# A projection product's bank goes back into the ring of accumulator banks two turns later

## The reference, cut to what matters

```python
proj = h @ w_in[l]                       # h: 512 x 1024
qkv = silu(centred_depthwise_conv(concat([qd, kd, vd]), dn_conv_w[l]))   # 5 taps along the sequence
qd, kd, vd = split(qkv)                  # 512 features each
qd = l2norm(qd per head) * DN_DK**-0.5
kd = l2norm(kd per head)
o  = bidir_gated_deltanet(qd, kd, vd, beta, g)     # 8 heads, chunks of 64
```

## Time and profile before

| | us |
|---|---|
| median of 3 runs | 3446.06 |
| lowest, highest | 3445.08, 3454.87 |
| the profiled execution | 3454.78 |
| its span, first to last instruction | 3453.0 |
| PE busy in it | 3298.4 (96%) |
| DVE busy | 1882.4 (55%) |
| ACT busy | 1437.2 (42%) |

### The profile page before, as it was taken

One profiled execution on the slowest core, in us unless ns is written; L12 is line 12 of the kernel. 1 busy time (PEld: TensorE's weight loads), 2 busy tenths in 40 slices (PEclk: granted clock), 3 DMA queues, 4 the chain that ended last, 5 costly groups with the idle time before them and its releaser, 6 DMA issues.

```text
span 3453.0 us, 61428 instructions
## 1 busy us (share of the span) xinstructions
PE 3298.4 (96%) x26780; PEld 2625.2 (76%) x26780; DVE 1882.4 (55%) x2834; ACT 1437.2 (42%) x2518; POOL 200.7 (6%) x188
## 2 busy tenths in 40 slices
PE   8899999999998999999999998989999999999999
PEld 6587887788875787878788876767788767677787
DVE  6565657756565565557755654453444644434444
ACT  5534224434255443234433454444433445444432
POOL 0041330000000232300000000000000000000000
PEclk9999999999999999999999998999999999999999
DMA  4001103232331011123223231201122312111222
GB/s 153 25 21 45 39 27 123 93 104 92 97 113 49 8 33 50 33 69 117 92 95 101 81 118 47 95 30 63 55 89 78 109 48 89 44 58 59 78 73 95
DMA packets 75212, 249.15 MB, mean 72 GB/s; under 512 B 9280, under 2 KB 10944, under 8 KB 73920
## 3 DMA queue, kind: packets, MB, share of 16 engines
q1 hardware_dynamic: 74944, 245.22, 21.7%
HBM read 237.88 MB, written 6.29 MB: 71 GB/s over the span
## 4 chain that ended last, share of the span: by engine, by line
PE 85%; DVE 7%; ACT 6%; issue 2%; DMA 0%; SPq 0%; ACTq 0%; DVEq 0%
PE psum L518 82%; PE psum L695 2%; ACT s_tmp L1247 1%; ACT s_w L1247 1%; DVE s_nm L2033 1%; DVE s_tmp L1954 1%; DVE s_ffy L1954 1%; DVE s_w L1951 1%; ACT s_E L1247 1%; DVE s_tmp L1951 1%; ACT L1247 0%; DVE s_xb L1951 0%; PE psum L605 0%; ACT L1259 0%; ACT s_ffy L1247 0%
## 5 line engine op out<-in xcount | busy, mean ns | idle before, releaser
L518 PE MATMUL psum<-s_h,s_w 128*128 128x512 f32 (+1 forms) x6864 | 1665.3, 399 | 30.5 <-DVE s_tmp L1954 18.0
L518 PEld LDWEIGHTS psum<-s_h,s_w 128*128 128x128 f32 (+1 forms) x6864 | 1288.0, 190 | 337.4 <-issue 46.5
L1951 DVE TENSOR_TENSOR s_w<-s_stage,s_w 128x1024 fp32r<-128x1024 f32 (+2 forms) x468 | 530.1, 1134 | 410.5 <-ACT s_w L1247 408.8
L1247 ACT ACTIVATE s_w<-s_stage 128x1024 fp32r<-128x1024 f32 (+2 forms) x468 | 451.3, 966 | 284.4 <-PE psum L518 263.4
L518 PE MATMUL psum<-s_ffa,s_w 128*128 128x512 f32 x1056 | 242.1, 390 | 4.6 <-DVE s_ffa L1951 4.6
L518 PEld LDWEIGHTS psum<-s_ffa,s_w 128*128 128x128 f32 x1056 | 197.8, 188 | 47.9 <-DVE s_ffa L1951 7.1
L518 PE MATMUL psum<-s_oR,s_w 128*128 128x512 f32 (+1 forms) x960 | 211.5, 371 | 0.0
L2033 DVE TENSOR_REDUCE s_nm<-psum 128x1 f32<-128x512 f32 (+3 forms) x288 | 138.2, 521 | 126.8 <-PE psum L518 126.2
L1247 ACT ACTIVATE s_E<-psum,s_nm 128x256 f32<-128x256 f32 (+3 forms) x224 | 114.3, 515 | 192.8 <-DVE s_nm L2033 192.8
L1954 DVE SCALAR_TENSOR_TENSOR s_ffy<-psum,s_pcol,s_ffy 128x511 f32<-128x511 f32 x176 | 131.7, 748 | 111.3 <-ACT s_ffy L1247 108.2
L1247 ACT ACTIVATE s_tmp<-psum 128x512 f32<-128x512 f32 (+2 forms) x154 | 87.5, 568 | 244.5 <-PE psum L518 239.3
(11 more groups left out here) (284 smaller groups left out, 3491.2 us busy)
## 6 DMA issues: line engine op xcount, KB each, us to landing
s_stage<-w SPq DMA_DIRECT2D x192, 512.0 KB, 3.3
s_stage<-wup SPq DMA_DIRECT2D x88, 512.0 KB, 3.2
s_stage<-wo SPq DMA_DIRECT2D x32, 512.0 KB, 3.3
s_stage<-wdn SPq DMA_DIRECT2D x32, 512.0 KB, 3.5
s_stage<-wdn SPq DMA_DIRECT2D x16, 384.0 KB, 3.1
spill<-s_x SPq DMA_DIRECT2D x2, 2048.0 KB, 8.9
s_stage<-woa SPq DMA_DIRECT2D x16, 256.0 KB, 2.7
s_x<-spill SPq DMA_DIRECT2D x2, 2048.0 KB, 7.9
```

Of the source, the lines that this page charges most:

```text
L518: return self.e.matmul(out, left, right, start=first, stop=last, skip_group_check=True)
L1247: return self.e.activation(out, src, func, **kw)
L1951: return self.e.tensor_tensor(out, a, b, op)
```

## The change

The call of `give` in PE's `project_begin` moves behind the two turns that follow the product. In this kernel these turns are empty for PE in that stream (other streams issue in them), and in the same turns ACT and DVE compute the taps. Nothing else is changed: no instruction is added or removed on any engine. What changes is which bank each later take pops, and with it the event that it waits for.

```diff
     def project_begin(self, key, hi, lo, ht):
         l, _, g, s3, j = key
         yield from self.lin_steps(key, self.d["w1"][l, 6 + 4 * s3 + 2 * g + j], 8, hi, lo, ht, 4)
+        yield
+        yield
         self.give(key, ("vec_proj", key, "y", 4))
-        yield
-        yield
```

More of the change, by code:

```diff
@@ L855, in project_begin @@
         yield from self.lin_steps(key, self.d["w1"][l, 6 + 4 * s3 + 2 * g + j], 8, hi, lo, ht, 4)
-        self.give(key, ("vec_proj", key, "y", 4))
         yield
         yield
+        self.give(key, ("vec_proj", key, "y", 4))
     def project_end(self, key):
```

## The result

| | before | after |
|---|---|---|
| median, us | 3448.16 | 3459.02 |
| lowest to highest | 3444.21 to 3456.79 | 3451.24 to 3463.08 |
| runs | 20 | 20 |
| ratio (95% interval) | | 1.0025 (1.0019 to 1.0031) |
| the profiled execution, its span | 3454.78, 3453.0 | 3459.46, 3457.7 |

The changed kernel is slower by a quarter of a per cent: 0.0025 x 3448 = 8.6 us (6.6 to 10.7), inside the 0.3% that the prediction counted as no change, but real by its interval. The profiled execution of before, at 3454.78, is one of the eight. The forecast was +7.

The account below looks back on a forecast made before the run. PE was taken as the bound, busy 3298.4 of 3453.0 us. Per layer +1.6 (first stage), 0 (third wait) and +1.9 (chain stage) gave +3.5, both layers +7.0, so median 3453, range 3444 to 3460.

Parts of the forecast that it names:

- First wait: First stage, product (2,0): PE waits for exponential e4 instead of a tap; of 4.08 us only 1.3 come back.
- The wait for kd0: First stage, squares' sum of (1,0): new PE wait of 5.7 us for DVE's kd0; next sum 3.4 us later.
- The clock after it: First stage, 12 product matmuls after the new kd0 wait: lower clock adds 1.5 us, making the second sum 4.9 late.
- Second wait: First stage, product (2,1): the 4.90 us wait stays, released by e8; start 0.1 to 1.6 us later, +1.6 taken.
- Third wait: First stage, score S14: starts 1.3 us earlier, but the transpose of (2,1) still waits for the silu; 0 us back.
- Chain stage: Group 1's (2,0) and (2,1) wait for the gate's tanh: 0.94 us lost at each, 1.9 us per layer.
- Sum: Whole kernel: +3.5 us per layer, +7.0 for both; profiled execution 3461.8 us, median 3453.
- A: First-stage waits go because e4 and e8 are done when PE arrives: at least 18 us gained, 3428; 7%.
- B: New waits at kd0 and the chain stage's tanh are absorbed: between -4 and +2 us, say 3446; 18%.
- C: Lag grows through two low-clock stretches per layer: +11.6 us or more, 3458 and above; 19%.
- D: Whole kernel: the change does nothing, as the takes meet the same events; no separate chance given.

Follow-up runs that it names:

- run 3: The kernel before with its own ring, plus an added PE wait for kd0 ahead of the squares' sum of (1,0); 3459.77 us, ratio 1.0027.
- run 5: Kernel before, with head group 0's projections giving their bank two turns later and the cum product's bank one turn later; 3442.85 us, ratio 0.9976.
- run 8: The change in both head groups, plus DVE's taps moved behind the row maxima in group 0; 3440.25 us, 0.9977 of the kernel before.
- run 2: Kernel before, with only head group 1's projections (chain stage) keeping their bank two more turns; 3458.68 us, ratio 1.0020.
- run 6: Kernel before with its own ring, all four DVE taps moved behind the row maxima in head group 0; 3425.82 us, ratio 0.9926.
- run 7: Kernel before, with each projection's bank given one turn later and group 0's DVE taps behind the row maxima; 3416.61 us, ratio 0.9903.
- run 4: Kernel before, with each projection's bank given back one turn later instead of the change's two; 3445.33 us, ratio 0.9978.

## Why the prediction was right, step by step

**First wait.** Predicted: 2.8 us, released by e4, 1.3 us gained. Measured: 2.87, released by ACT s_x, 0.83 and 1.25 gained. Right; in layer 0 the wait was shorter by 1.21, and 0.4 of that was lost at a wait just before it (ACT s_ktok, 1.20 instead of 0.80).

**The wait for kd0.** Predicted: at the squares' sum of (1,0), 5.7 us, released by the subtraction into s_sckd. Measured: 5.46 idle in both layers, and the sum's distance from (2,0) grew by 5.74 and 6.16, where the forecast's 111.4 - 94.75 against 106.99 - 96.07 is 5.73. Right; the 0.4 more in layer 1 is product (2,0) at the lower clock, and run 3 shows that this one wait makes the kernel before as slow as the change, run 5 that moving the one bank takes the loss away.

**The clock after it.** I added 1.5 us, from a group of 12 matmuls after a wait of 4.90. In layer 0 the sum and the 12 after it took 2.07 and 4.49 us instead of 1.02 and 3.33. The rows overlap, so their lengths don't add; from the one sum to the next it was 115.67 - 110.25 = 5.42 us instead of 3.78, 1.6 more. In layer 1:

```profile
1105.39 2.07 PE L518 MATMUL psum<-s_tmp,s_cst 128*128 128x512 f32 x2 [5.46 <-DVE s_sckd L1951]
1106.47 5.22 PE L518 MATMUL psum<-s_h,s_w 128*128 128x512 f32 x12
...
1122.86 4.32 PE L518 MATMUL psum<-s_h,s_w 128*128 128x512 f32 x12 [3.67 <-ACT s_x L1247]
```

Here the 12 took 5.22, and the way to the next sum 6.14, 2.4 more. The granted clock of the two stretches, changed kernel, layer 0 (columns as in the earlier trace rows):

```profile
106.70:113.50 6.80, 3.25 (x6) 1.92 (x7) 3.08 (x8) 5.97 (x13) 0.00 (x0) 0.52 0.21 77
126.99:131.50 4.51, 4.51 (x13) 3.29 (x13) 3.83 (x7) 4.48 (x8) 0.00 (x0) 0.62 0.00 0
```

0.52 means nearly all of it at 1.2 GHz. The wait began at 104.79, and from there to 106.70 the granted clock was still 1.00, so it fell while PE was idle. This term was right to 0.1 us in layer 0 and short by 0.9 in layer 1. The Trainium skill says on the page TensorE: Matmul & The Clock Gate (Part 1) that the gate's window runs free of the kernel's start. The runs agree as far as they go: the same 5.46 us is followed by 12 matmuls in 4.49 in one layer and in 5.22 in the other, and in run 8 in 5.09.

**Second wait.** Predicted: stays, released by e8, (2,1) 0.1 to 1.6 us later, 1.6 taken. Measured: 3.67 us, released by ACT s_x, and (2,1) later by +2.32 and +3.05 (sums of the first four lines of the table). The releaser and the sign are right; the size is above the value taken and below the upper bound of 3.9. In layer 0 most of the 0.7 is the first wait's smaller gain, in layer 1 the 1.45 is the clock, 0.4 before the wait for kd0 and 0.9 after it. The cover that the forecast took off was right too, though its 1.95 is 2.05 by the rows it names (117.79 - 115.74). Its lower bound is likewise off by 0.3: an undisturbed product takes 5.74 us, not two groups of 3.02, whose rows overlap.

**Third wait.** Predicted: S14 earlier, and T takes it up, 0 us come back. Measured: 1.51 + 2.51 = 4.02 us in layer 0, where there had been 2.58 + 1.43 = 4.01. Exactly so. The sum up to T went from 2.32 to 2.37 in layer 0 and from 3.05 to 2.53 in layer 1; the 0.5 there is the 12 matmuls of (2,1), 4.32 us instead of 5.07, so clock and not waiting.

**Chain stage.** Predicted: a gap of 0.94 at each of two places a layer, released by the tanh, 1.9 a layer. Measured: four gaps of 0.78 of idle time. Between the starts of the two groups of 12 lie 324.08 - 320.29 = 3.79 us where before the second group began about half of 5.74 after the first, so the step itself grew by 0.9, as forecast, and the row behind each product came 1.06 to 1.10 later; with what little else moved, 2.2 a layer. The place and the cause are right, and run 2 has them by themselves. What the forecast lacked is the stretch at 1.2 GHz that follows behind the chain stage, 1.4 to 1.6 us a layer: it said that everything after the first stage "only moves with it". By the traces this is the largest term that the sum left out.

**Sum.** 7.0 predicted; 9.3 by the distances of the stages alone, 8.6 (6.6 to 10.7) by the timings. With the 2.9 us behind the chain stages and the 2.8 that layer 1 gained back behind T the sum for the first pair of profiles is 9.4; these two, of which the forecast had neither, cancel, and that is luck. The profiled execution was forecast at 3461.8 and took 3459.46, also by help of the second block (3.5 us less). The predicted median of 3453 stood on the 3446.06 of three runs; twenty gave 3448.16, 2.1 more. The rest of the 6 us to 3459.02 is 1.6 of the terms and 2.3 by which the medians lie further apart than the means. The measured median lies 1 us below the range's upper end, in the part that was added for wandering medians.

**Rivals.** A (the waits go) did not come about, and for the reason stated: the maxima stood behind the first taps. Runs 6 and 7 show that A's condition was the right one, and that in another ring it was worth more than A's 18 us once met. In the changed kernel itself (run 8) the waits for s_x fell from 16.1 to 0.3 us, but kd0 and the tanh kept their price and 7.9 us were gained on before. B (absorbed, -4 to +2) lies below the interval's lower end of 6.6. C is only just told apart: its time of 3458 and above holds the measured median of 3459.02, its cost of +11.6 or more lies above the interval's upper end of 10.7. Its cause, the low clock, is what my terms were short of. D is refuted by the waits.

The Trainium skill's page Perfetto Trace Analysis (section Matmul Optimizations) wants all 8 PSUM banks in use; held against the runs this is not enough. Holding each bank out of the ring for one turn used fewer of them and gained (0.9978), holding it out for two lost (1.0025). The count of banks does not decide here; the event with which the bank at the front comes back does, and the measurement goes before the rule.

## What to carry to other kernels

A ring of buffers handed out in order waits for the buffer at its front even if others are free, so where a buffer is given back decides who waits for what; write the order of takes and gives down and look up the end of each event before moving one, as a shift by one turn and by two had opposite signs. When a wait only gets shorter and has a new releaser, follow that one engine further: here the first taps of two products in front of a row maximum on DVE cost more than any order of the ring. Price a removed or an added stall of PE with the clock after it, since it was nearly half of the best version's gain in the stages touched (13.7 of 29.6 us), and look for it in stretches far behind the stall as well. When two profiles are compared, cut them at the same instruction first: here up to 10.7 us of busy time differed where the programs did not.

## What the runs showed of the hardware that was not expected

- The clock follows the small waits closely. Over a whole execution the mean granted clock was 0.983 before, 0.986 in run 4, 0.989 in run 6 and 0.992 in run 7, which is (1 - 0.983) x 2 x 3453.0 = 117 us at 1.2 GHz in the first and 55 us in the last. Up to the matmul at 2075.86, each step of removed waiting brought PE's busy time down as well: -2.0 us with -5.5 of idle (run 4), -7.2 with -13.5 (run 6), -13.7 with -15.9 (run 7).
- It works in the other direction too: the change added 2.9 us of idle and 5.3 of busy time there, run 2 3.6 and 5.6, run 3 4.1 and 2.9. A microsecond of waiting added or removed moved the busy time by 0.2 us (run 5) to 1.8 us (the change). What sets the factor stays open; two profiles of before differ by 2.2 us of busy time there, so the small ones are rough.
- A stretch of one program with the same waits took 194.2 us in both profiles of before and 190.8 in both of the change (from the matmul at 2075.86 in before to that at 2270.10).
- An idle time of 0.78 us on PE grew the step from matmul to matmul by 0.94 us (1.17 instead of 0.23) and moved the row behind the product by 1.06 to 1.10 at full clock, eight times in two executions.
